# The 80-row tile of six projections computed in four column groups of TensorE

## The chip, the cores and the metric

One core of a Trainium2 chip runs the whole program in one launch. The metric is the device time of that launch in microseconds, the median of several runs. The core has five engines that run side by side and meet only at semaphores: TensorE (PE in the rows, PEld its weight loads), VectorE (DVE), ScalarE (ACT), GpSimd (POOL) and SyncE (SP, which here only starts DMA transfers). TensorE multiplies a stationary operand, up to 128 columns wide, with a moving one of up to 512 columns, and writes to PSUM, 128 partitions by 8 banks of 512 fp32; the stationary operand's columns become the output's partitions. VectorE and ScalarE take results from PSUM to SBUF.

## What is computed

The reference runs two layers of a streaming encoder over 592 tokens: 512 of a prompt, 64 of a sample and 16 meta tokens. Only the parts around the change are shown.

```python
def even_mixer(x, ...):                       # layer 0
    z = jnp.einsum('btd,de->bte', x, w_in)    # D_MODEL = 1024
    hq, hf, hi, hg, fq, fk, fv, ffg = jnp.split(z, [...], axis=-1)
    ...
    o_hg = rms_norm(o_hg, hg_norm_g).reshape(B, T, HG_VO) * jax.nn.sigmoid(hg)
    ...
    mixed = jnp.concatenate([o_hg, o_fox.reshape(B, T, FOX_W).astype(o_hg.dtype)], axis=-1)
    y = jnp.einsum('bte,ed->btd', mixed, w_out)
...
def trunk(...):
    for l in range(DEPTH):                    # DEPTH = 2
        ...                                   # y from even_mixer or odd_mixer (its w_out alike)
        x = layer_norm(ALPHA * x + y.astype(x.dtype), p['ln_mix_g'][l], p['ln_mix_b'][l])
        f = moe(x, ...)
        x = layer_norm(ALPHA * x + f, p['ln_ffn_g'][l], p['ln_ffn_b'][l])
```

Everything is fp32. Here `hi` (called v in the kernel), `hg` (g), `fk` and `fv` are 592 x 512 each with a contraction over 1024, and each of the two output projections (one a layer) is 592 x 1024 over 1024.

## The kernel before

**Tiles.** The 592 tokens are held feature-major in `xT` (128 partitions, 8 chunks of features, 592 tokens) and are cut into five token tiles, `TILES = [128, 128, 128, 128, 80]`. Tile 4, the 80 rows, holds the sample's 64 tokens and the 16 meta tokens.

**Token-major projections.** For v, g, fk and fv, `to_tokens` (L1067 to L1075) takes the tokens of a tile as the stationary operand and 512 columns of the weights as the moving one, and sums over 8 chunks: 8 matmuls to a tile, each of which is two records in the trace. The output projection of layer l, in `out_and_experts` (L1311), does the same for two halves of 512 columns into two banks (L1324); after tile i it transposes tile i - 1, which has been normalized by then (`normed_tile`).

**Order.** Each engine runs its own list as written. TensorE: the first forget projection, v tiles 0 to 4, the first q projection (L1084), g tiles 0 to 4; then 20 units of the recurrence with the other feature-major projections laid between them (L1190), before which it waits until g tiles 3 and 4 and v tile 4 are out of PSUM; then fk tiles, each followed by the transposes of the tile before (L1225); fv tiles; attention of layer 0, which waits for fv tile 4; the output projection; the router; 13 blocks of experts. Each block (`gate_up` L1420, `down` L1441) already multiplies in four column groups: four experts have 32 slots each, the stationary operand is 32 columns wide, and the output goes to partitions 32j to 32j + 31. Layer 1 has latent attention in between and then `out_and_experts(1)`.

**PSUM.** The eight banks are four pairs, and a ticket for each result says in which pair it lies. `claim` waits until the pair's last user has been read (`ps_free`), `filled` until TensorE is done (`pe_full`).

**Who empties PSUM.** ScalarE copies v (L1670), fk (L1665) and fv (L1720), and takes exp(-x) of g (L1678), one instruction for each tile. VectorE adds the residual to an output projection straight from PSUM, 1024 columns in one instruction (L2107, `stt` in `layer_norm_tile`), then takes the statistics and scales (L2110 to L2117); GpSimd computes the inverse root in between (L843, L844). SyncE starts the weight loads: the g weights when v tile 4 is done, experts 2 and 3 and part of 4 when tile 4 of the output projection is done.

## Time and profile before

| | us |
|---|---|
| median of 3 runs | 1290.17 |
| lowest and highest | 1289.34, 1294.49 |
| the profiled execution | 1288.5 |
| its span, first to last instruction | 1285.5 |
| TensorE busy (share of the span) | 1137.2 (88%) |
| VectorE | 568.5 (44%) |
| ScalarE | 263.5 (20%) |
| GpSimd | 221.2 (17%) |

The rows in the section after the next give times in microseconds from the span's start. A row of the timeline or of the chain stands for several instructions (x16: sixteen); its second number runs from the start of the first to the end of the last. The end of a matmul is modelled, and matmuls are pipelined: one of 512 columns is shown 0.59 us long while the next one starts after 0.43. In the shape 128*80 of a matmul the first number is the rows of the array that take part, the second the columns, that is the tokens.

### The profile page before, as it was taken

The page shows a single profiled execution, that of the slowest core. Times are in us where ns is not written, and L with a number is a line of the kernel's source. Part 1 is how long each engine was busy: PE and PEld are TensorE (multiplying, and loading weights), DVE is VectorE, ACT ScalarE, POOL GpSimd, SP SyncE. Part 2 cuts the span into 40 slices and gives each one's busy share as a digit, 9 for nine tenths or more (in the row PEclk, how much of TensorE's full clock was granted, in tenths as well). Part 3 has the DMA queues.
Part 4 walks back from the last instruction along what each step waited for, and adds up shares of the span by engine and source line. Part 5 has one row for each costly group of instructions (what it writes and reads, how often), then busy time and mean ns, then how long its engine had stood idle before and what let it go on. Part 6 is the DMA issues. An engine that isn't in the chain of part 4 may idle for free.

```text
span 1285.5 us, 16760 instructions
## 1 busy us (share of the span) xinstructions
PE 1137.2 (88%) x6333; PEld 611.3 (48%) x6333; DVE 568.5 (44%) x1254; ACT 263.5 (20%) x622; POOL 221.2 (17%) x382
## 2 busy tenths in 40 slices
PE   8999999999899939999839899999999975999965
PEld 4547777644654313333215446677574432333322
DVE  2079878610734435643365230450253344474226
ACT  1214334311420001111101312332331010111012
POOL 0106444421101211001062300000000210100114
PEclk9999999999999959999959999999999996999987
DMA  9103211261842277999582312000104246899935
GB/s 351 66 30 146 87 67 66 83 226 53 70 165 98 104 292 288 376 416 337 204 312 78 118 61 66 1 1 1 66 1 196 93 171 246 303 396 405 331 108 201
DMA packets 41821, 214.69 MB, mean 167 GB/s; under 512 B 4488, under 2 KB 6088, under 8 KB 32400
## 3 DMA queue, kind: packets, MB, share of 16 engines
q1 hardware_dynamic: 24288, 152.57, 30.4%
q0 software_dynamic: 17168, 60.27, 15.1%
q8 instruction: 51, 0.84, 0.3%
q10 hardware_dynamic: 288, 0.80, 0.2%
q14 instruction: 26, 0.21, 0.1%
HBM read 180.31 MB, written 33.29 MB: 166 GB/s over the span
## 4 chain that ended last, share of the span: by engine, by line
PE 79%; DVE 8%; issue 4%; DMA 4%; ACT 3%; POOL 1%; DVEq 0%; ACTq 0%; POOLq 0%; SPq 0%
PE pair L1420 12%; PE pair L1324 11%; PE pair L1073 11%; PE pair L1441 6%; PE pair L1084 5%; PE pair L1190 5%; PE pair L1256 5%; PE pair L1517 3%; PE pair L1293 3%; PE pair L1569 2%; DMA arena<-x_rows,ints 2%; PE pair L1406 2%; PE pair L1114 2%; PE pair L1549 2%; PE pair L1291 2%
## 5 line engine op out<-in xcount | busy, mean ns | idle before, releaser
L1073 PE MATMUL pair<-ring,xT 128*128 128x512 f32 (+1 forms) x320 | 138.8, 593 | 0.0
L1420 PE MATMUL pair<-ring,arena 128*32 128x512 f32 x608 | 130.2, 598 | 0.0
L1420 PE MATMUL pair<-arena 128*32 128x512 f32 x736 | 106.0, 631 | 8.1 <-issue 4.6
L1073 PEld LDWEIGHTS pair<-ring,xT 128*128 128x128 f32 (+1 forms) x320 | 57.7, 182 | 75.5 <-issue 75.1
L1190 PE MATMUL pair<-xT,ring 128*128 128x296 f32 x320 | 85.1, 421 | 6.1 <-ACT arena L1607 3.0
L843 POOL TENSOR_SCALAR small<-small 128x1 f32<-128x1 f32 (+3 forms) x45 | 17.2, 383 | 414.2 <-DVE small L2112 359.1
L865 POOL TENSOR_TENSOR arena<-arena 128x128 f32<-128x128 f32 x140 | 57.2, 443 | 155.4 <-PE pair L1116 86.6
L1256 PE MATMUL pair<-arena 128*128 128x264 f32 (+5 forms) x280 | 76.5, 402 | 2.6 <-issue 1.4
L2048 DVE TENSOR_REDUCE small<-pair 128x1 f32<-128x144 f32 (+4 forms) x40 | 22.4, 560 | 120.3 <-PE pair L1261 120.2
L1324 PE MATMUL pair<-ring,mixT 128*128 128x512 f32 (+1 forms) x160 | 72.1, 593 | 1.0 <-issue 1.0
L1190 PEld LDWEIGHTS pair<-xT,ring 128*128 128x128 f32 x320 | 60.4, 193 | 25.6 <-issue 9.2
L991 POOL DMA_INDIRECT arena<-x_rows,ints x26 | 26.4, 1014 | 268.6 <-PE pair L1406 164.6
L1324 PE MATMUL pair<-ring,xT 128*128 128x512 f32 (+1 forms) x160 | 71.9, 592 | 0.0
L2250 DVE COPY arena<-pair 128x256 f32<-128x256 f32 x26 | 11.0, 423 | 134.9 <-PE pair L1429 134.9
L1441 PE MATMUL pair<-ring,arena 128*32 128x512 f32 x304 | 65.3, 595 | 4.0 <-DVE arena L2250 4.0
L1420 PEld LDWEIGHTS pair<-arena 128*32 128x32 f32 x736 | 31.1, 116 | 68.6 <-issue 68.6
L1084 PE MATMUL pair<-arena,ring 128*128 128x296 f32 (+1 forms) x224 | 62.1, 438 | 0.0
L1420 PEld LDWEIGHTS pair<-ring,arena 128*32 128x32 f32 x608 | 34.0, 111 | 57.4 <-issue 57.4
L1517 PE MATMUL pair<-ring,xT 128*128 128x512 f32 (+3 forms) x160 | 59.2, 526 | 1.1 <-ACT xT L1598 1.1
L1420 PE MATMUL pair<-xT,arena 128*32 128x512 f32 x320 | 56.3, 592 | 0.0
L1598 ACT COPY xT<-pair 128x1024 f32<-128x1024 f32 (+1 forms) x15 | 14.2, 948 | 202.9 <-PE pair L1065 202.9
L2107 DVE SCALAR_TENSOR_TENSOR rb<-xr,pair 128x1024 f32<-128x1024 f32 (+1 forms) x10 | 12.2, 1221 | 95.8 <-PE pair L1324 95.8
(356 smaller groups left out, 1910.4 us busy)
## 6 DMA issues: line engine op xcount, KB each, us to landing
arena<-in_moe_w_gate_up SPq DMA_DIRECT2D x14, 2048.0 KB, 9.2
ring<-in_moe_w_gate_up SPq DMA_DIRECT2D x12, 2048.0 KB, 9.4
arena<-in_moe_w_down SPq DMA_DIRECT2D x14, 1024.0 KB, 9.6
y_rows<-arena SPq DMA_DIRECT2D x26, 512.0 KB, 8.5
ring<-in_moe_w_down SPq DMA_DIRECT2D x12, 1024.0 KB, 11.6
xT<-in_moe_w_gate_up SPq DMA_DIRECT2D x6, 2048.0 KB, 15.0
ring<-in_even_w_in SPq DMA_DIRECT2D x5, 2048.0 KB, 7.5
y_rows<-xr POOLq DMA_DIRECT2D x12, 512.0 KB, 8.6
```

Source lines behind the costliest of these rows:

```text
L865: last = pool.tensor_tensor(dst, both, mid, ALU.subtract)
L991: pool.indirect_dma_start(xg[:, e % 2, :], None, x_rows[2 * l], bass.IndirectOffsetOnAxis(ap=sloti[:, e:e + 1], axis=0)).then_inc(xg_in[e ...
L1073: last = pe.matmul(ps[0:P, 0:n], xT[:, k, 128 * i:128 * i + P], w[:, k, :], start=(k == 0), stop=(k == chunks - 1))
L1084: last = pe.matmul(ps[0:w.shape[2], 512 * s:512 * s + n], w[:, k, :], src[:, k, n * s:n * s + n], start=(k == 0), stop=(k == chunks - 1))
L1114: pe.matmul(ps[0:P, 128 * n:128 * n + P], gbuf[:, u % 2, n, 0:P], gbuf[:, u % 2, n, 0:P], start=True, stop=True)
L1190: last = pe.matmul(ps[0:w.shape[2], 512 * s:512 * s + n], w[:, k, :], xT[:, k, n * s:n * s + n], start=(k == 0), stop=(k == KD - 1))
L1256: last = pe.matmul(ps[0:P, lo:lo + cols], q_, k_, start=(c == 0), stop=(mask is None and c == len(lq) - 1))
L1293: last = pe.matmul(out, vb[j], pT[:, n % 2, 128 * j:128 * j + P], start=False, stop=(j == nb - 1))
L1324: last = pe.matmul(ps[0:P, 512 * half:512 * half + 512], mixed(k, i), w[:, k, :], start=(k == 0), stop=(k == KD - 1))
L1420: last = pe.matmul(bank[c, :], xgT[:, e % 2, k, c], expert_place(x)[0][:, k, :], start=(k == 0), stop=(k == KD - 1))
L1441: last = pe.matmul(psum[2][c:c + 32, 512 * half:512 * half + 512], hT[:, e % 2, 128 * k + c:128 * k + c + 32], expert_place(x)[1][:, k, 51 ...
L1517: last = pe.matmul(ps[0:P, lo:lo + n], xT[:, k, 128 * i:128 * i + P], w[:, k, :], start=(k == 0), stop=(k == KD - 1))
```

## The change

Tile 4 of the six projections v, g, fk, fv and the two output projections is multiplied in four column groups of 32. Its rows are cut into 0 to 31, 32 to 63 and 64 to 79 (`ROWS`). Groups 0 to 2 take one of these each and multiply it with the first three quarters of the weight's columns, 384 of 512. Group 3, whose output is on the partitions from 96 on, takes the last 128 columns for all three in turn; the result of row group r goes to columns 128r to 128r + 127 of the same bank (`moved`). For each chunk k the program issues one matmul for each of groups 0 to 2 and three for group 3, which counts through its own 24 pairs of row group and chunk. Other tiles stay as they are. The results are collected by four instructions where there was one: the 384 columns of all 80 rows, and three blocks of 128 columns from partition 96 on to the rows where they belong. For an output projection each of the four covers both halves.

```diff
+        ROWS = [(0, 32), (32, 64), (64, TILES[4])]
+
+        def moved(ps, r, lo=0, n=512):
+            a, b = ROWS[r]
+            return ps[96:96 + b - a, lo + n // 4 * r:lo + n // 4 * (r + 1)]
...
+            def last_tile(ps, w, tokens, lo=0):
+                K, n = w.shape[1], w.shape[2]
+                m = 3 * n // 4
+                for k in range(K):
+                    for a, b in ROWS:
+                        pe.matmul(ps[a:b, lo:lo + m], tokens(k)[:, a:b], w[:, k, 0:m],
+                                  start=(k == 0), stop=(k == K - 1))
+                    for t in range(3 * k, 3 * k + 3):
+                        r, c = divmod(t, K)
+                        a, b = ROWS[r]
+                        last = pe.matmul(moved(ps, r, lo, n), tokens(c)[:, a:b], w[:, c, m:n],
+                                         start=(c == 0), stop=(c == K - 1))
+                return last
...
+                if i == NT - 1:
+                    last_tile(ps, w, lambda k: xT[:, k, 128 * i:128 * i + P]).then_inc(pe_full.sem(key), 1)
+                    return
...
                     for half, w in ((0, w0), (1, w1)):
+                        if i == NT - 1:
+                            last = last_tile(ps, w, lambda k: mixed(k, i), 512 * half)
+                            continue
...
+            def token_rows(f, out, ps, i):
+                if i < NT - 1:
+                    return f(out, ps[0:128, 0:512])
+                f(out[:, 0:384], ps[0:TILES[i], 0:384])
+                for r, (a, b) in enumerate(ROWS):
+                    last = f(out[a:b, 384:512], moved(ps, r))
+                return last
...
-                copy(fks[0:P, i, :], filled(act, key)[0:P, 0:512]).then_inc(ps_free.sem(key), 1)
+                token_rows(copy, fks[0:P, i, :], filled(act, key), i).then_inc(ps_free.sem(key), 1)
...
-                stt(r, xr[0:P, b, :], ALPHA, filled(dve, key)[0:P, :], ALU.mult, ALU.add).then_inc(ps_free.sem(key), 1)
+                ps = filled(dve, key)
+                if i < NT - 1:
+                    added = stt(r, xr[0:P, b, :], ALPHA, ps[0:P, :], ALU.mult, ALU.add)
+                else:
+                    halves = lambda v: v.rearrange("p (h n) -> p h n", h=2)
+                    stt(halves(r)[:, :, 0:384], halves(xr[0:P, b, :])[:, :, 0:384], ALPHA,
+                        halves(ps[0:P, :])[:, :, 0:384], ALU.mult, ALU.add)
+                    for q, (lo, hi) in enumerate(ROWS):
+                        added = stt(halves(rb[lo:hi, b, :])[:, :, 384:512], halves(xr[lo:hi, b, :])[:, :, 384:512], ALPHA,
+                                    halves(ps[96:96 + hi - lo, :])[:, :, 128 * q:128 * q + 128], ALU.mult, ALU.add)
+                added.then_inc(ps_free.sem(key), 1)
```

The copies of v and fv and the exp of g go through `token_rows` as that of fk does. The places as they stand in the built programs follow; a shape is that of the output, and line numbers of the changed kernel are its own.

TensorE, tile 4 of v, between the other tiles of v (`ring` holds the weights, `xT` the tokens) and the q projection, before:

```order
L1095 MATMUL pair<-xT,mixT 128x296 x16
L1073 MATMUL pair<-ring,xT 128x512 x32
L1073 MATMUL pair<-ring,xT 80x512 x8
L1084 MATMUL pair<-xT,mixT 128x296 x16
L1073 MATMUL pair<-ring,xT 128x512 x32
```

The same place in the changed kernel, from chunk 5 on, where group 3 goes over to the 16 rows (in the five chunks ahead the rows of L1086 are one, `32x128 x3`):

```order
L1081 MATMUL pair<-ring,xT 32x384 x2
L1081 MATMUL pair<-ring,xT 16x384
L1086 MATMUL pair<-ring,xT 32x128
L1086 MATMUL pair<-ring,xT 16x128 x2
L1081 MATMUL pair<-ring,xT 32x384 x2
L1081 MATMUL pair<-ring,xT 16x384
L1086 MATMUL pair<-ring,xT 16x128 x3
L1081 MATMUL pair<-ring,xT 32x384 x2
L1081 MATMUL pair<-ring,xT 16x384
L1086 MATMUL pair<-ring,xT 16x128 x3
L1109 MATMUL pair<-xT,mixT 128x296 x16
```

The 8 matmuls of the tile have become 48, six to a chunk, at the same place in the list.

ScalarE, the exp of g tile 4 and what is behind it (L1636 is the exp of the recurrence's decays), before:

```order
L1636 ACTIVATE arena<-arena 128x896
L1678 ACTIVATE arena<-pair 128x512 x4
L1678 ACTIVATE arena<-pair 80x512
L1636 ACTIVATE arena<-arena 128x896 x2
L1645 COPY arena<-pair 80x128
```

And in the changed kernel:

```order
L1673 ACTIVATE arena<-arena 128x896
L1715 ACTIVATE arena<-pair 128x512 x4
L1715 ACTIVATE arena<-pair 80x384
L1715 ACTIVATE arena<-pair 32x128 x2
L1715 ACTIVATE arena<-pair 16x128
L1673 ACTIVATE arena<-arena 128x896 x2
```

Four instructions stand where one did, and the decays of the next unit are queued behind them.

VectorE, the residual sum and the statistics of tile 4 after an output projection, before:

```order
L2117 SCALAR_TENSOR_TENSOR rb<-rb,small,lng 128x1024
L2107 SCALAR_TENSOR_TENSOR rb<-xr,pair 80x1024
L2110 BN_STATS small<-rb 80x6
L2111 BN_STATS small<-rb 80x6
L2112 BN_AGGR small<-small 80x2
```

And in the changed kernel:

```order
L2165 SCALAR_TENSOR_TENSOR rb<-rb,small,lng 128x1024
L2150 SCALAR_TENSOR_TENSOR rb<-xr,pair 80x2x384
L2153 SCALAR_TENSOR_TENSOR rb<-xr,pair 32x2x128 x2
L2153 SCALAR_TENSOR_TENSOR rb<-xr,pair 16x2x128
L2158 BN_STATS small<-rb 80x6
```

The sum comes in four pieces, and the statistics wait for the last.

## Rows read from the trace of the kernel before

**Rows 1.** The page: busy time of TensorE; the chain that ended last, by engine

```profile
PE 1137.2 (88%) x6333; PEld 611.3 (48%) x6333; DVE 568.5 (44%) x1254; ACT 263.5 (20%) x622; POOL 221.2 (17%) x382
...
PE 79%; DVE 8%; issue 4%; DMA 4%; ACT 3%; POOL 1%; DVEq 0%; ACTq 0%; POOLq 0%; SPq 0%
```

**Rows 2.** The chain in order of time: start us, us, what

```profile
16.13 34.37 PE pair L1073 x80
...
276.06 6.88 PE pair L1073 x16
...
429.85 13.75 PE pair L1324 x32
443.72 1.23 DVE rb L2107
```

**Rows 3.** Timeline between two expert blocks: start us, us, engine, line, instructions

```profile
606.06 1.04 PE L1420 MATMUL pair<-ring,arena 128*32 128x512 f32 x8
...
607.03 0.44 PE L1429 MATMUL pair<-cst,arena 128*128 128x128 f32 x2
...
607.30 1.04 PE L1406 MATMUL pair<-cst,arena 128*128 128x128 f32 x8
...
608.27 0.63 PE L1441 MATMUL pair<-arena 128*32 128x512 f32 x3
...
608.29 0.62 PE L1441 MATMUL pair<-ring,arena 128*32 128x512 f32 x1
608.30 0.12 PEld L1441 LDWEIGHTS pair<-arena 128*32 128x32 f32 x3
...
608.73 0.60 PE L1441 MATMUL pair<-arena 128*32 128x512 f32 x3
```

**Rows 4.** Short passes: one group by shape, then timelines, L1167 in two windows

```profile
L1293 PE MATMUL pair<-arena 128*128 128x128 f32 x240 | 34.9, 275 | 0.8 <-issue 0.8
...
368.30 0.72 PE L1293 MATMUL pair<-arena 128*128 128x128 f32 x5
...
1054.75 0.28 PE L1167 MATMUL pair<-xT,vecs 128*32 128x80 f32 x4 [0.78 <-ACT xT L1598]
...
1054.75 0.48 PE L1167 MATMUL pair<-xT,vecs 128*32 128x80 f32 x16 [0.78 <-ACT xT L1598]
...
104.72 0.39 PE L1134 MATMUL pair<-arena 80*16 80x128 f32 x2
```

**Rows 5.** Reads of PSUM by ScalarE and VectorE: groups by shape, then timelines

```profile
L1747 ACT COPY arena<-pair 128x128 f32<-128x128 f32 x12 | 3.1, 256 | 0.5
...
282.96 0.58 ACT L1665 COPY arena<-pair 80x512 f32<-80x512 f32 x1 [6.23 <-PE pair L1073]
283.44 0.58 ACT L1715 COPY arena<-pair 128x512 f32<-128x512 f32 x1
...
746.64 0.42 DVE L2418 TENSOR_TENSOR arena<-pair,cst 128x256 f32<-128x256 f32 x1 [1.15 <-PE pair L1549]
746.99 0.41 DVE L2419 TENSOR_TENSOR arena<-pair,cst 128x256 f32<-128x256 f32 x1
```

**Rows 6.** Timeline of TensorE behind g tile 4 and fk tile 4

```profile
93.64 4.22 PE L1190 MATMUL pair<-xT,ring 128*128 128x296 f32 x16 [0.83 <-ACT arena L1678]
...
284.17 0.47 PE L1225 MATMUL pair<-cst,arena 80*128 80x80 f32 x4 [0.81 <-ACT arena L1715]
```

**Rows 7.** Timeline of TensorE: the transposes of tile 4 behind the output projection

```profile
449.76 0.77 PE L1065 MATMUL pair<-cst,rb 80*128 80x80 f32 x8 [0.51 <-DVE rb L2117]
```

**Rows 8.** The chain again: gate and up of the first expert block, and a later one

```profile
474.88 8.79 PE pair L1420 x64
...
600.23 6.87 PE pair L1420 x64
```

**Rows 9.** Windows: stretch; PE, PEld, DVE, ACT, POOL busy; PEclk, DMA, GB/s

```profile
474.90:478.30 3.40, 3.40 (x17) 0.91 (x21) 0.00 (x0) 0.00 (x0) 0.32 (x1) 0.50 0.46 154
...
600.30:606.90 6.60, 6.60 (x64) 1.82 (x56) 0.69 (x1) 0.58 (x1) 1.05 (x2) 1.00 0.97 318
```

More of the change, by code:

```diff
@@ L1669, in _ @@
                 P = TILES[i]
-                copy(hv[0:P, i, :], filled(act, ("v", i))[0:P, 0:512]).then_inc(ps_free.sem(("v", i)), 1)
+                token_rows(copy, hv[0:P, i, :], filled(act, ("v", i)), i).then_inc(ps_free.sem(("v", i)), 1)
                 if i == 1:
@@ L1677, in _ @@
                 P, key = TILES[i], ("g", i)
-                act.activation(hgate[0:P, i, :], filled(act, key)[0:P, 0:512], ACT.Exp, scale=-1.0).then_inc(ps_free.sem(key), 1)
+                token_rows(lambda out, ps: act.activation(out, ps, ACT.Exp, scale=-1.0), hgate[0:P, i, :],
+                           filled(act, key), i).then_inc(ps_free.sem(key), 1)
             for u in range(20):
@@ L1719, in _ @@
                     act.wait_ge(*vz_sb["fox"])
-                copy(fv[0:P, i, :], filled(act, key)[0:P, 0:512]).then_inc(ps_free.sem(key), 1)
+                token_rows(copy, fv[0:P, i, :], filled(act, key), i).then_inc(ps_free.sem(key), 1)
             def att_exp(n):
```

## The prediction

> **What bounds the kernel now.** I read the page first, for which engine the end of the run hangs on, then the chain of waits in order of time, for where the six projections lie in it, then the timeline around the expert blocks, because they are the only work before the change that multiplies in four column groups. TensorE is busy 88% of the span and 79% of the chain that ended last is its work [rows 1]. The chain runs through tile 4 of all six projections: v, g and fv each stand in it as one unbroken piece of 80 records, 34.4 us, fk as five of 16, and tile 4 of an output projection (both halves of the columns) ends a piece of 13.75 us that hands straight over to VectorE [rows 2]. With the halves that makes eight times 512 columns. So time taken from TensorE in tile 4 comes off the run, less what the engine that empties PSUM needs more.
>
> Each fp32 matmul is two records in the trace, which I call passes. The old tile 4 of one projection half is 8 chunks x 2 passes = 16 passes of 512 columns, and takes 6.88 us, 0.429 us a pass, with 80 of 128 columns of the array in use [rows 2]. A tile of 128 rows takes the same time, so the 48 idle columns are what the change goes for.
>
> **TensorE, one projection half.** After the change three groups of 32 columns (the last with 16 rows) hold the tile's rows and take 384 of the 512 weight columns, and the fourth group takes the other 128 for the three row groups in turn. Groups 0 to 2 have 16 passes of 384 columns: 0.429 x 384/512 = 0.322 us each, 5.15 us. Group 3 has 8 x 3 x 2 = 48 passes of 128 columns. The price of such a pass decides the case. Five passes of 128 columns in a row end 0.72 us after the first one starts, and one lasts 0.275, so they start 0.111 apart; eight transposes give (1.04 - 0.27)/7 = 0.110 [rows 3, 4]. Those are full-width passes. In column groups the nearest thing is the router's partial sums, four groups at once, 80 columns: 4 passes take 0.28 us and 16 take 0.48, so three further rounds cost 0.20, 0.067 each, which is 80/512 of 0.429 [rows 4]. So loading 32 new columns of weights does not show even in a pass shorter than ours. I take 0.109 (128/512 of 0.429 and 2 ns). Below it there is only the bare 0.107; above it stands the pair of 128-column passes with a 16-column load, the first after a wait, 0.39 - 0.27 = 0.12 apart [rows 4]. Group 3 is then the longest with 48 x 0.109 = 5.24 us, and one half costs 5.24 in place of 6.87.
>
> Entering and leaving column groups costs too. The last round of the gate and up weights starts at 606.49 (two rounds of 0.43 from 606.06), the next full-width pass would start at 606.92 and does so at 607.03; the last of the eight transposes starts at 608.07 and the next round of column groups at 608.27, not 608.18. That is 0.11 less the 0.02 by which the groups of a round lie apart, and 0.09: 0.09 each way [rows 3]. The Trainium skill (TensorEngine Tiling (Array Packing), Key Properties) says that a change of tiling mode drains the engine; the trace agrees.
>
> Do four groups of unlike length run side by side? In the built program the two passes of a matmul stand together, group after group. Yet at 608.27 the first passes of all four groups start within 0.02 us and the second ones follow 0.46 later [rows 3]: a group's second pass waits while later matmuls of other groups go ahead. The changed stream needs this to reach a few instructions further, since group 3 must start its second matmul while the second passes of the others still wait. If it reached no further than now, group 3 would fall behind once, by part of a chunk, and catch up in its own time: the wide groups leave it no gap.
>
> **The engines that empty PSUM.** For v, g, fk and fv ScalarE makes four instructions of one. 80x512 takes 0.58 and 128x128 takes 0.256, so 384 columns take 0.47, and the four take 0.47 + 3 x 0.256 = 1.24, or 1.24 - 3 x 0.10 = 0.94 if they overlap as the copies at 282.96 and 283.44 do, which lie 0.48 apart at 0.58 long [rows 5]. I take +0.36, at most +0.66. After v nothing waits for it: TensorE has q to do. After g TensorE waits 0.83 for this instruction now [rows 6], so all of it is on the path. After fk the next copy is behind it in ScalarE's queue, and TensorE waits for that copy, 0.81 [rows 6]: on the path. After fv the attention waits for it in the same way: on the path.
>
> For the output projections VectorE makes four of one. 80x1024 takes 1.22. 256 columns take 0.42, so a column costs (1.22 - 0.42)/768 = 1.04 ns, 768 columns 0.95, and the four 0.95 + 3 x 0.42 = 2.22. Instructions of 256 columns that read PSUM start 0.33 to 0.35 apart at 0.42 long [rows 5], so the four take some 1.94. I take +0.72, at most +1.0. It is on the path: VectorE starts at 443.72, when TensorE ends tile 4, and TensorE later waits 0.51 for the normalized tile [rows 2, 7]. That wait also says that TensorE's own work in between (tile 3's transposes and router sums) is 0.5 us short of binding; it moves forward by more than VectorE's, so it stays hidden.
>
> **The sum.** v: 6.87 - 5.24 - 0.19 = 1.44 saved. g: the way out of column groups falls into a wait, 6.87 - 5.24 - 0.09 - 0.36 = 1.18. fk: 1.44 - 0.36 = 1.08. fv as g, 1.18. Each output projection: 13.74 - 10.48 - 0.09 - 0.72 = 2.45, twice 4.90. Together 9.8 us. The profiled execution took 1288.5 us (span 1285.5), so it would be 1278.7; against the median of the runs, 1290.17, it is **1280.4 us**. The DMA loads behind tile 4 (the g weights behind v, experts 2 and 3 behind the output projection) are started by the tile's end and move with it, so I count nothing for them. The unknowns: ScalarE and VectorE up to 1.5 us more; a 0.001 us change of the narrow pass is 48 x 8 x 0.001 = 0.38 us, so 0.12 would give back 4.2. Then there is TensorE's clock. The granted clock is 0.50 (1.2 of 2.4 GHz) while the first expert block begins, straight behind the router's long waits, and 1.00 in a later one; that first block costs 8.79 us where a later one costs 6.87 [rows 8, 9]. It is the first of five such pieces in the chain. Work that arrives earlier may meet the return of the clock sooner or later than now; each can move by up to the 1.9 us that it costs, and I allow 3 us either way in total.
>
> **Rivals.** *The narrow passes are not free of their loads.* Nowhere in this kernel does one group load weights three times while the other three are in one pass. If in group 3 each load (0.11 [rows 3]) comes before its pass and not beside the one before, a pass costs 0.22, a half 48 x 0.22 = 10.5, and the run gets 8 x (10.5 - 5.24) = 42 us longer than my sum: about **1322 us**. It decides from 0.109 + 9.8/384 = 0.134 us a pass on: dearer than that, the change loses. Against it: at 608.30 the loads for the second passes start 0.03 after the first passes have [rows 3], and the 0.067 rounds. The Trainium skill (TensorE: Matmul & The Clock Gate, Part 3) states that a weight load overlaps a running matmul only where the row groups differ, and here they never do; by that rule this rival would be the forecast, and the load at 608.30 speaks against the rule.
>
> *Passes start strictly in the program's order.* Then a chunk is a wide pass, three times one more beside the next group's first, and six narrow ones behind: 3 x 0.322 + 5 x 0.109 = 1.51 us, a half 12.1, and 8 x (12.1 - 5.24) = 55 on top of my sum: about **1335 us**. By the same order the gate and up block would take 8 x 4 x 0.429 = 13.7 us, and it takes 6.87 [rows 8]. The Trainium skill (the same page and part) says that matmuls start and end in program order with no reordering; that rule gives this rival, and the 6.87 denies it.
>
> *Part of it comes off.* Narrow passes at 0.12 to 0.13, or a short stall at each chunk because group 3 runs ahead or behind, or the clock comes back later after a router: with a pass of 0.12 (4.2) and 1.4 from the clock on 1280.4 it is **1286 us**, within 0.5% of before.
>
> **How the numbers follow.** About 0.5% is what a measurement of this kernel can tell from no change; it is 6.45 us, the forecast is 9.8. The sum as made has 0.68, and 0.62 of it ends more than 0.5% faster, the rest is lost to the clock's share. Part of it comes off has 0.18. The serial loads have 0.10, strict order 0.04. So faster 0.62, same 0.24, slower 0.14. The range runs from 1280.4 less 5 (clock, and overlaps better than taken) to 1290, which takes in the third rival and a narrow pass of nearly 0.13; what is left out is mainly the two rivals beyond it.
>
> **What would show it.** The timeline of tile 4 of v: 96 records of TensorE in about 5.4 us, the narrow ones 0.109 apart, the wide ones 0.32; a gap at every eighth part would be the third rival, narrow ones 0.22 apart the first. In the chain of waits v's piece shortens from 34.37 to about 32.9 us and the piece of 13.75 to about 10.6. TensorE's wait before L1190 near 92 us grows from 0.83 to about 1.2, and VectorE needs about 1.9 us from the end of an output projection to the statistics. I am wrong if these hold and the total does not fall, which could only be later waits (for expert weights, or the clock) that grow by the same.

## The result and the profile after

The changed kernel takes **1280.19 us**, the kernel before, run on the same chips, 1292.44: a ratio of 0.9915 with an interval of 0.9892 to 0.9939, 11.0 us less (7.9 to 14.0). The forecast was 1280.4, which was 9.8 us less than the 1290.17 of the three runs of before known then; the range was 1275.5 to 1290. The profiled execution took 1280.19 as well, its span is 1277.3 (1285.5 before).

The page of the changed kernel, busy time and the chain by engine (before: [rows 1]):

```profile
PE 1125.8 (88%) x6973; PEld 632.0 (49%) x6973; DVE 570.7 (45%) x1260; ACT 266.7 (21%) x634; POOL 223.3 (17%) x382
...
PE 77%; DVE 9%; issue 5%; DMA 5%; ACT 3%; SPq 1%; POOL 0%; DVEq 0%; ACTq 0%; POOLq 0%
```

TensorE is busy 11.4 us less with 640 records more. The timeline of TensorE at the start and the end of tile 4 of v (start us, us, engine, line, instructions) shows that the four groups run side by side:

```profile
43.26 0.59 PE L1098 MATMUL pair<-ring,xT 128*128 128x512 f32 x1
43.78 0.52 PE L1081 MATMUL pair<-ring,xT 128*32 128x384 f32 x3
43.80 0.52 PE L1086 MATMUL pair<-ring,xT 128*32 128x128 f32 x3
44.13 0.49 PE L1081 MATMUL pair<-ring,xT 128*16 128x384 f32 x3
44.15 0.49 PE L1086 MATMUL pair<-ring,xT 128*32 128x128 f32 x3
...
48.74 0.49 PE L1086 MATMUL pair<-ring,xT 128*16 128x128 f32 x3
49.16 8.24 PE L1109 MATMUL pair<-xT,mixT 128*128 128x296 f32 x32
```

Rounds of wide passes start at 43.78, 44.13 and from there 0.322 apart; beside each stand three narrow ones of group 3. Three narrow passes last 0.49 from first start to last end and one lasts 0.27, so they start 0.11 apart. The tile takes 49.16 - 43.78 = 5.38 us, the way out of column groups in it; the old one took 6.87 [rows 2]. The way in is 43.78 - 43.26 - 0.43 = 0.09. All four token-major tiles that take part show 5.38, and the output projection 10.62 where it had 13.75 [rows 2] (from 426.74 to the transposes at 437.36, in the rows further down).

What ScalarE needs behind g, and TensorE's waits behind g, fk and fv, from the timeline of the changed kernel (the first two waits answer to [rows 6]):

```profile
90.92 1.34 ACT L1715 ACTIVATE arena<-pair 80x384 f32<-80x384 f32 x4 [4.78 <-PE pair L1086]
...
92.56 0.74 PE L1215 MATMUL pair<-xT,ring 128*128 128x296 f32 x2 [1.67 <-ACT arena L1715]
...
282.43 0.47 PE L1250 MATMUL pair<-cst,arena 80*128 80x80 f32 x4 [1.49 <-ACT arena L1753]
...
317.63 0.48 PE L1281 MATMUL pair<-arena 128*128 128x144 f32 x2 [1.85 <-ACT arena L1634]
```

The waits were 0.83, 0.81 and, behind fv, 1.14 (at 320.15 in the trace of the kernel before); they have grown by 0.84, 0.68 and 0.71, where the forecast put 0.36 on each.

The chain of waits has a piece that the kernel before doesn't have, the load of the g weights behind v (chain in order of time: start us, us, what; the tile of v stands between the first two rows):

```profile
16.11 27.73 PE pair L1098 x64
...
49.26 8.47 DMA ring<-in_even_w_in
57.77 27.73 PE pair L1098 x64
```

### The profile page after: what moved, and what is told of

Its sections match the earlier page's. It is cut to its first block, busy times and chain, and to the rows that moved or that the text cites. A ratio compares the mean times of both kernels' runs of the same rounds, so it can differ in the third digit from the quotient of the medians.

```text
span 1277.3 us, 18058 instructions
## 1 busy us (share of the span) xinstructions
PE 1125.8 (88%) x6973; PEld 632.0 (49%) x6973; DVE 570.7 (45%) x1260; ACT 266.7 (21%) x634; POOL 223.3 (17%) x382
## 4 chain that ended last, share of the span: by engine, by line
PE 77%; DVE 9%; issue 5%; DMA 5%; ACT 3%; SPq 1%; POOL 0%; DVEq 0%; ACTq 0%; POOLq 0%
PE pair L1448 12%; PE pair L1098 9%; PE pair L1352 9%; PE pair L1469 6%; PE pair L1215 5%; PE pair L1109 5%; PE pair L1281 5%; PE pair L1545 4%; PE pair L1318 3%; PE pair L1597 2%; PE pair L1086 2%; DMA arena<-x_rows,ints 2%; PE pair L1434 2%; PE pair L1139 2%; DMA ring<-in_even_w_in 2%
## 5 line engine op out<-in xcount | busy, mean ns | idle before, releaser
L1098 PE MATMUL pair<-ring,xT 128*128 128x512 f32 x256 | 111.3, 593 | 0.9 <-DMA ring<-in_even_w_in 0.9
L1098 PEld LDWEIGHTS pair<-ring,xT 128*128 128x128 f32 x256 | 48.1, 190 | 59.8 <-issue 57.9
L1215 PEld LDWEIGHTS pair<-xT,ring 128*128 128x128 f32 x320 | 60.4, 193 | 25.8 <-issue 9.4
L1352 PE MATMUL pair<-ring,mixT 128*128 128x512 f32 x128 | 57.7, 593 | 1.0 <-issue 1.0
L1352 PE MATMUL pair<-ring,xT 128*128 128x512 f32 x128 | 57.5, 592 | 0.0
L1109 PEld LDWEIGHTS pair<-arena,ring 128*128 128x128 f32 x224 | 42.4, 190 | 18.1 <-issue 6.7
```

Source lines behind the costliest of these rows:

```text
L1098: last = pe.matmul(ps[0:P, 0:n], xT[:, k, 128 * i:128 * i + P], w[:, k, :], start=(k == 0), stop=(k == chunks - 1))
L1109: last = pe.matmul(ps[0:w.shape[2], 512 * s:512 * s + n], w[:, k, :], src[:, k, n * s:n * s + n], start=(k == 0), stop=(k == chunks - 1))
L1215: last = pe.matmul(ps[0:w.shape[2], 512 * s:512 * s + n], w[:, k, :], xT[:, k, n * s:n * s + n], start=(k == 0), stop=(k == KD - 1))
L1352: last = pe.matmul(ps[0:P, 512 * half:512 * half + 512], mixed(k, i), w[:, k, :], start=(k == 0), stop=(k == KD - 1))
```

## The experiments

Where a median is given, it stands beside that of the kernel before in the same job, and the interval is of the ratio. Line numbers are each kernel's own.

**e1: the four input projections alone.** Tile 4 of the output projections is as before.

```diff
-                        if i == NT - 1:
-                            last = last_tile(ps, w, lambda k: mixed(k, i), 512 * half)
-                            continue
...
-                if i < NT - 1:
+                if True:
                     added = stt(r, xr[0:P, b, :], ALPHA, ps[0:P, :], ALU.mult, ALU.add)
```

> Only v, g, fk and fv have their tile 4 in column groups; the two output projections are as before. My theory (each tile gives back its own passes less its emptying, and nothing else): the profile of the changed kernel shows 1.4 us off at v, 0.7 at g, 0.65 at fk and 0.8 at fv, 3.5 in all, against 4.9 in my sum; the time should fall by 3 to 5 us. Rival (the gain is not in the tiles but in how later work meets TensorE's clock and the expert weights): the time falls by 8 us or more, or not at all, and not in step with the tiles.

Measured: 1288.52 against 1290.17, 0.9988 (0.9968 to 1.0007): 1.6 us less, 4.1 less to 0.9 more. The stages in the trace have their gain: tile 4 takes 5.38, and TensorE begins to transpose tile 3 of fk at 280.31 where it began at 282.76. So the question was whether something later takes the gain; e11 takes it up.

**e2: the output projections alone.**

```diff
-                if i == NT - 1:
-                    last_tile(ps, w, lambda k: xT[:, k, 128 * i:128 * i + P]).then_inc(pe_full.sem(key), 1)
-                    return
...
-                if i < NT - 1:
-                    return f(out, ps[0:128, 0:512])
+                if True:
+                    return f(out, ps[0:TILES[i], 0:512])
```

> Only the two output projections have their tile 4 in column groups. My theory: 2.1 us off each by the changed kernel's trace (2.45 in my sum), 4 to 5 us in all; with the run that has only v, g, fk and fv it adds up to the whole change. Rival (later waits give the gain): the two parts do not add up to the 11 us measured for the whole, or one of them has it all.

Measured: 1284.20 against 1290.17, 0.9937 (0.9914 to 0.9961): 8.1 us less (5.0 to 11.1; the medians lie 6.0 apart), where my sum had 4.9 for this part. It looks like more than I had counted, if only just outside the interval, and e12 and e13 ask why.

**e4: the narrow passes behind all wide ones.** How far ahead of waiting matmuls does a free group go?

```diff
                 for k in range(K):
                     for a, b in ROWS:
                         pe.matmul(ps[a:b, lo:lo + m], tokens(k)[:, a:b], w[:, k, 0:m],
                                   start=(k == 0), stop=(k == K - 1))
-                    for t in range(3 * k, 3 * k + 3):
-                        r, c = divmod(t, K)
...
+                for t in range(3 * K):
+                    r, c = divmod(t, K)
...
```

> The same 96 passes a tile half, but all wide ones of groups 0 to 2 are issued first and the 48 narrow ones of group 3 behind them. It tells how far TensorE looks past passes that wait. My theory (the reach is limited, some 10 to 20 passes): the narrow ones start only when the wide ones are nearly through, so a half takes 5.2 + 5.2 us less some 1 to 2 us of overlap at the end, 8.4 to 9.4 in place of 5.3, and the kernel is 25 to 33 us slower than the changed one, 14 to 22 slower than before. Rival 1 (the reach is far, each group has its own list): no difference from the changed kernel. Rival 2 (strict order between groups, which only looks concurrent where groups alternate): a half takes 10.4 and the kernel is 41 us slower than the changed one.

Measured: 1312.35 against 1290.17, 1.0163 (1.0127 to 1.0199). TensorE's timeline in tile 4 of v:

```profile
43.73 0.52 PE L1081 MATMUL pair<-ring,xT 128*32 128x384 f32 x3
...
47.30 0.81 PE L1081 MATMUL pair<-ring,xT 128*32 128x384 f32 x6
47.65 0.51 PE L1086 MATMUL pair<-ring,xT 128*32 128x128 f32 x3
...
53.00 0.52 PE L1109 MATMUL pair<-xT,mixT 128*128 128x296 f32 x1
```

Group 3 stands idle until 47.65. At 47.62 the thirteenth of the 16 rounds of wide passes has started, and within 0.03 us the first narrow pass starts. So three rounds, nine wide passes, were still waiting when a matmul behind them could go. Nine is not the whole rule, though. In the output projection of e4 the wide passes of the second half stand behind the 48 narrow ones of the first:

```profile
449.88 0.71 PE L1086 MATMUL pair<-ring,xT 128*16 128x128 f32 x5
450.32 0.52 PE L1081 MATMUL pair<-ring,mixT 128*32 128x384 f32 x3
450.42 0.49 PE L1086 MATMUL pair<-ring,xT 128*16 128x128 f32 x3
```

Here groups 0 to 2 stand idle until only three narrow passes wait, and in layer 1 it is the same (1059.40, three narrow ones from 1059.50 on). One reading fits both counts: a matmul can go when no group ahead of it has more than three passes waiting, three times three in tile 4 of v and once three here. The counts are measured, the reading per group is an inference from them. The tile of v takes 9.27 us, 3.89 more than in the changed kernel; over four tiles and two output projections (18.02 against 10.62) that is 30.4 us, and the medians of the two kernels lie 32.2 apart. A group does go ahead of others that wait, but only so far, and the close interleaving by chunk in the changed kernel is what the gain hangs on.

**e5: three groups, nothing moved.** Groups 0 to 2 take all 512 columns, the fourth stays empty.

```diff
                     for a, b in ROWS:
-                        pe.matmul(ps[a:b, lo:lo + m], tokens(k)[:, a:b], w[:, k, 0:m],
+                        last = pe.matmul(ps[a:b, lo:lo + n], tokens(k)[:, a:b], w[:, k, :],
                                   start=(k == 0), stop=(k == K - 1))
-                    for t in range(3 * k, 3 * k + 3):
...
```

> Three column groups with all 512 columns each and no fourth group: nothing is moved to partition 96, and PSUM is emptied by one instruction as before. It has the column groups' own cost and none of the gain. My theory (the gain is only that 384 columns take the place of 512): each tile costs 16 x 0.429 us and 0.09 us at each change of mode, so the kernel is 1 us slower than before at most, no difference that can be measured. Rival (column groups are faster in themselves, for instance by shorter weight loads): it keeps a good part of the 11 us.

Measured: 1292.64 against 1290.17, 1.0019 (0.9997 to 1.0041). Tile 4 of v runs from 43.86 to 50.85, 6.99 us:

```profile
43.34 0.59 PE L1093 MATMUL pair<-ring,xT 128*128 128x512 f32 x1
43.86 0.62 PE L1081 MATMUL pair<-ring,xT 128*32 128x512 f32 x3
...
50.85 0.52 PE L1104 MATMUL pair<-xT,mixT 128*128 128x296 f32 x1
```

The way in is again 43.86 - 43.34 - 0.43 = 0.09, and the way out 6.99 - 6.87 = 0.12. Six visits cost 1.3 us, so column groups by themselves give nothing; the gain is the 128 columns that go to the fourth.

**e6: passes of 64 columns in group 3.** 96 passes in place of 48, with the same columns in all.

```diff
-                    for t in range(3 * k, 3 * k + 3):
-                        r, c = divmod(t, K)
+                    for t in range(6 * k, 6 * k + 6):
+                        rq, c = divmod(t, K)
+                        r, q = divmod(rq, 2)
+                        c0, c1 = (n - m) // 2 * q, (n - m) // 2 * (q + 1)
```

> Group 3 does the same columns in 96 passes of 64 columns to a tile half in place of 48 of 128. It measures the floor under a narrow pass. My theory (weight loads hide beside the pass before, in a group of its own too): 0.054 to 0.058 us a pass, group 3 stays at 5.2 to 5.6 us a half and the time within 2 us of the changed kernel. Rival (a load of 32 columns, shown 0.11 us long, bounds a pass from somewhere between 64 and 128 columns on): up to 0.11 a pass, 10.5 us a half, and 40 us longer in all.

Measured in one run: 1280.71, beside a median of 1289.52 for the kernel before. TensorE's timeline:

```profile
43.97 0.49 PE L1081 MATMUL pair<-ring,xT 128*32 128x384 f32 x3
44.00 0.50 PE L1088 MATMUL pair<-ring,xT 128*32 128x64 f32 x6
```

One such pass lasts 0.22, so six in 0.50 start 0.056 apart: 64/512 of 0.429 is 0.054, and 2 ns. The whole tile takes 5.50 in place of 5.38, 0.0025 us for each pass more. A weight load that is twice as frequent does not show, so the rival of serial loads is out, with a factor of two to spare.

**e8: finer pieces on ScalarE and VectorE.** The forecast let each piece begin before the one ahead was done. The trace of the changed kernel denied it, so here the 384 columns are copied in three pieces, each moved block in two, and VectorE's 768 columns in two.

```diff
-                f(out[:, 0:384], ps[0:TILES[i], 0:384])
+                for q in range(3):
+                    f(out[:, 128 * q:128 * q + 128], ps[0:TILES[i], 128 * q:128 * q + 128])
                 for r, (a, b) in enumerate(ROWS):
-                    last = f(out[a:b, 384:512], moved(ps, r))
+                    for c in (0, 64):
+                        last = f(out[a:b, 384 + c:448 + c], moved(ps, r)[:, c:c + 64])
...
+                    for o in (0, 512):
+                        stt(r[:, o:o + 384], xr[0:P, b, o:o + 384], ALPHA, ps[0:P, o:o + 384], ALU.mult, ALU.add)
```

> Pieces cut finer, with the same data: ScalarE takes the 384 columns as three of 128, and each moved block as two of 64; VectorE takes the 384 columns of the two halves as two instructions. It asks why the pieces did not overlap as I took them to (0.27 apart at 0.26 long on ScalarE, 0.96 at 0.95 on VectorE), while the rope products of another stage start 0.34 apart at 0.42 long. Guess 1 (a change of the first partition between source and destination, 96 to 0, stops the overlap): the three of 128 columns that stay on their partitions start about 0.16 apart, the moved ones do not overlap. Guess 2 (a change of the partitions from one instruction to the next stops it): the second of two moved ones with the same partitions starts early, the others do not. Guess 3 (fewer than 128 partitions stop it): none overlaps.

Measured in one run: 1277.69, beside 1289.52. First ScalarE behind v, then VectorE behind the output projection, from the timeline of e8:

```profile
49.26 0.59 ACT L1633 COPY arena<-pair 80x128 f32<-80x128 f32 x3 [4.79 <-PE pair L1086]
49.86 0.32 ACT L1636 COPY arena<-pair 32x64 f32<-32x64 f32 x2
...
50.19 0.32 ACT L1636 COPY arena<-pair 32x64 f32<-32x64 f32 x2
...
438.65 1.02 DVE L2153 SCALAR_TENSOR_TENSOR rb<-xr,pair 80x384 f32<-80x384 f32 x2 [5.13 <-PE pair L1086]
439.68 1.29 DVE L2155 SCALAR_TENSOR_TENSOR rb<-xr,pair 32x256 f32<-32x256 f32 x3
```

Three copies of 0.264 that write the same 80 partitions take 0.59: they start 0.16 apart. Two of 0.20 to the same 32 rows take 0.32: 0.11 apart. But the next pair, which reads the same PSUM partitions and writes other rows, starts at 50.19, when the one ahead is over (49.86 + 0.32 = 50.18). VectorE is alike: two sums of 0.547 over the same rows take 1.02, 0.47 apart; three of 0.42 to three different row ranges take 1.29, 0.43 apart. So the pieces that keep their first partitions overlap, and those that change one do not. The step from the wide copies to the first block changes only the first partition that is read (0 to 96; both write from row 0), the step from block to block on ScalarE only the one that is written, and either is enough. The length of the range does not decide it: the copies at 282.96 and 283.44 write 80 and 128 rows, both from 0, and overlap [rows 5]. The moved blocks always change one. The Trainium skill (VectorE: DVE Perf Modes, The DRAIN you can't avoid) says that an operation of VectorE does not start until the one ahead has emptied the pipe, but that one which is not held starts earlier. By the section that it points to, Two Vector instructions with no wait between them, an operation is held when an input or its output starts in another group of 32 partitions than in the instruction ahead. VectorE's starts agree with that: 0.47 apart at 0.55 long within the same groups, 0.43 apart at 0.42 long across them.

**e7: half of the residual sum early.** VectorE sums the first 512 columns while TensorE multiplies the second, which go to the other bank.

```diff
+                            if half == 0:
+                                last.then_inc(wo_half.sem, 1)
...
+                    dve.wait_ge(*wo_half[l])
+                    for h in range(2):
+                        if h == 1:
+                            filled(dve, key)
+                        o = 512 * h
+                        stt(r[:, o:o + 384], xr[0:P, b, o:o + 384], ALPHA, ps[0:P, o:o + 384], ALU.mult, ALU.add)
+                        for q, (lo, hi) in enumerate(ROWS):
+                            added = stt(rb[lo:hi, b, o + 384:o + 512], xr[lo:hi, b, o + 384:o + 512], ALPHA,
+                                        ps[96:96 + hi - lo, o + 128 * q:o + 128 * q + 128], ALU.mult, ALU.add)
```

> VectorE sums the first half (512 columns) of an output projection's tile 4 while TensorE multiplies the second, with a signal of its own: eight pieces in place of four, four of them behind the end. My theory (the pieces lie on the path): behind TensorE's end remain 0.55 + 3 x 0.29 = 1.4 us in place of 2.25, so the router begins 0.85 us earlier in each layer and the time falls by some 1.7 us, seen in the trace and hardly in the medians. Rival (TensorE's transposes and router sums of the other tiles are as late): nothing changes at the transposes of tile 4, whose wait for VectorE goes below 0.6 us.

Measured: 1278.15 against 1289.52, 0.9920 (0.9896 to 0.9944). VectorE is done 1.49 us behind TensorE's tile in place of 2.29, and the wait for tile 4's transposes is back to 0.52 [rows 7]; the total is the changed kernel's within the interval. So 0.8 us less on VectorE, twice, bought nothing that shows in four runs.

**e9: the moved blocks early too.** e7, and for v, g, fk and fv the first two row blocks of group 3 go to the second bank of the pair. ScalarE takes them when two thirds of the tile are done.

```diff
+        def placed(ps, r):
+            a, b = ROWS[r]
+            o = 512 + 128 * r if r < 2 else 0
+            return ps[96:96 + b - a, o:o + 128]
...
+                        if done and t == 2 * K - 1:
+                            last.then_inc(done, 1)
...
+                act.wait_ge(*early[key[0]])
+                for r, (a, b) in enumerate(ROWS):
+                    if r == 2:
+                        filled(act, key)
+                    last = f(out[a:b, 384:512], placed(ps, r))
+                return f(out[:, 0:384], ps[0:TILES[i], 0:384])
```

> Group 3 finishes its first two row blocks after two thirds of the tile. Here they are written to the second bank of the pair and their copies (v, fk, fv) and exp (g) run while TensorE is on the third; for an output projection VectorE sums the first half while TensorE multiplies the second. Left on the path behind a tile: for ScalarE one block and the 384 columns, two instructions whose partitions differ, so without overlap 0.26 + 0.48 = 0.74 us in place of 1.29; for VectorE 0.55 + 3 x 0.30 = 1.49 in place of 2.29. Theory (these engines' time behind a tile is on the path, as the four waits show): g, fk and fv 0.55 each and two output projections 0.8 each, 3.2 us less than the changed kernel, about 1277 where that has 1280. TensorE's tile stays at 5.38 us. Rival (it is off the path or the early reads disturb TensorE's passes): the same time as the changed kernel or more, and a half of a tile longer than 5.38.

Measured: 1277.08 against 1289.19, 0.9900 (0.9881 to 0.9918). In its timeline behind g ScalarE has two instructions left and TensorE waits 1.01 where the changed kernel waits 1.67:

```profile
90.71 0.77 ACT L1728 ACTIVATE arena<-pair 16x128 f32<-16x128 f32 x2 [0.78 <-PE pair L1092]
...
91.68 0.49 PE L1223 MATMUL pair<-xT,ring 128*128 128x296 f32 x1 [1.01 <-ACT arena L1728]
```

TensorE's tiles stay at 5.38, so the early reads cost it nothing. The 0.66 (behind fv 0.60, 1.52 against 2.12 from the last start) are there in the trace; their sum of under 2 us does not show in the total.

**e10: the changed kernel again**, as it is, in the same job.

> The changed kernel as it is, beside e9 and e11, since a few microseconds are to be told apart. Both theories: 0.9915 of the kernel before, within its interval of 0.9892 to 0.9939.

Measured: 1277.52 against 1289.19, 0.9902 (0.9882 to 0.9921). e9 is 0.4 us below it. The means lie 0.3 apart, and by the scatter of their 5 and 6 runs I estimate some 2.4 us of doubt either way: the expected 3.2 are not there, but the up to 2 us of the three ScalarE waits could be, unseen.

**e11: the kernel of e1 again.**

> The kernel of e1 once more: v, g, fk and fv in four groups, the output projections as before. It came out only 1.6 us faster, where the stages sum to some 4. Theory (the stages keep their gain, and the rest was TensorE's clock, whose mean was 0.950 in e1's runs against 0.953 of the kernel before): runs of equal mean clock are 4 to 5 us apart, and the median is 2 to 5 us below that of before, 0.996 to 0.998. Rival (a later wait takes the gain of the inputs): again 1.6 us or less, at an equal clock too.

Measured: 1284.70 against 1289.19, 0.9967 (0.9956 to 0.9979), 4.3 us less (2.7 to 5.7). A straight line through each kernel's runs (span over mean granted clock) puts e11 at a clock of 0.950 4.0 us and e1 4.9 us below the kernel before of the same job; against one line through the kernel before of all jobs it is 5.5 and 3.4. The inputs keep their gain. That e1 showed only 1.6 goes with a lower mean clock in its runs, 0.950 against 0.953; why its runs had it is not shown.

**e12 and e13: VectorE longer.** The first statistics of tile 4 are computed four times more in the changed kernel, once more in the kernel before; nothing else changes.

```diff
                 st = lst[0:P, b, :]
+                if i == NT - 1:
+                    for _ in range(4):
+                        chain(dve.bn_stats(st[:, 0:6], src[:, 0:512]))
```

> The changed kernel, with VectorE's first statistics of tile 4 computed four more times behind each output projection, some 0.7 us each, 2.9 us more on VectorE; the result is the same. Theory (cover that ends): TensorE goes on from the end of tile 4 to the first rows of the experts in 28.65 us in the kernel before and in 28.65 and 28.29 in the changed one, whose VectorE is 1.0 longer there, because the rows are gathered behind 9.4 MB of weights that start when tile 4 ends and last 24 us. In the changed kernel the weights end just as the gather is issued (462.1 and 463.1 us), so the cover is used up: the stretch grows by 2.4 to 2.9, to 30.7 to 31.5, in both layers. Rival 1 (VectorE is covered further): it stays under 29.1. Rival 2 (VectorE is on the path, as the prediction had it): it grows by the full 2.9.

> The kernel before, with the first statistics of tile 4 computed once more behind each output projection, some 0.7 us more on VectorE; the result is the same. Theory (the weights that start with the end of tile 4 cover it): from the end of tile 4 to the first rows of the experts TensorE takes the 28.65 us of the kernel before (28.1 to 29.1 in all kernels so far). Rival (VectorE is on the path, as the prediction had it): 29.35 in layer 0 and 29.3 in layer 1.

Measured: e12 1283.67 against 1287.24, 0.9955 (0.9936 to 0.9974); e13 1291.86, 1.0021 (1.0003 to 1.0040). What they were made for is the stretch from the end of tile 4 to the first rows of the experts. Timelines of TensorE and GpSimd there: the kernel before, the changed kernel, e12.

```profile
443.42 1.04 PE L1065 MATMUL pair<-cst,rb 128*128 128x128 f32 x8
...
468.23 0.97 POOL L991 DMA_INDIRECT arena<-x_rows,ints  x1 [0.68 <-DVE ints L2223]
...
472.07 0.45 PE L1406 MATMUL pair<-cst,arena 128*128 128x128 f32 x1 [4.71 <-DMA arena<-x_rows,ints]
```

```profile
426.74 0.52 PE L1081 MATMUL pair<-ring,mixT 128*32 128x384 f32 x3
...
437.36 1.09 PE L1072 MATMUL pair<-cst,rb 128*128 128x128 f32 x8
437.57 0.95 DVE L2150 SCALAR_TENSOR_TENSOR rb<-xr,pair 80x768 f32<-80x768 f32 x1 [5.13 <-PE pair L1086]
438.53 1.29 DVE L2153 SCALAR_TENSOR_TENSOR rb<-xr,pair 32x256 f32<-32x256 f32 x3
...
444.66 0.77 PE L1072 MATMUL pair<-cst,rb 80*128 80x80 f32 x8 [1.42 <-DVE rb L2165]
...
463.12 0.97 POOL L998 DMA_INDIRECT arena<-x_rows,ints  x1 [0.69 <-DVE ints L2271]
...
466.00 0.45 PE L1434 MATMUL pair<-cst,arena 128*128 128x128 f32 x1 [3.76 <-DMA arena<-x_rows,ints]
```

```profile
438.90 1.09 PE L1072 MATMUL pair<-cst,rb 128*128 128x128 f32 x8
...
468.12 0.97 POOL L998 DMA_INDIRECT arena<-x_rows,ints  x1 [0.69 <-DVE ints L2274]
...
471.10 0.45 PE L1434 MATMUL pair<-cst,arena 128*128 128x128 f32 x1 [3.85 <-DMA arena<-x_rows,ints]
```

From these and their like, in us from the start of tile 3's transposes, layer 0 and layer 1 (the second gather is that of the rows of the first experts):

| kernel | tile 4's transposes | second gather issued | TensorE has the rows |
|---|---|---|---|
| before | 6.34, 6.34 | 24.81, 24.53 | 28.65, 28.56 |
| e13 | 7.07, 7.07 | 25.42, 25.54 | 28.86, 28.36 |
| changed | 7.31, 7.31 | 25.76, 25.78 | 28.65, 28.57 |
| changed again, e10 | 7.31, 7.31 | 25.49, 25.83 | 28.29, 28.64 |
| e9 | 6.41, 6.40 | 24.89, 24.74 | 28.46, 28.34 |
| e2 | 7.31, 7.31 | 26.34, 26.09 | 29.06, 28.90 |
| e12 | 10.22, 10.21 | 29.22, 29.22 | 32.20, 31.85 |

With the gather issued anywhere from 24.5 to 25.8 the rows are there at 28.3 to 28.9 (28.1 to 29.2 with e6 and e7); from 26 on they come later with it, 2.6 to 3.0 us behind. Windows of the same stretch (stretch; PE, PEld, DVE, ACT, POOL busy; PEclk, DMA share, GB/s), of the kernel before, the changed one and e12, show what holds the early ones up:

```profile
443.40:468.00 24.60, 7.56 (x94) 4.86 (x92) 17.14 (x59) 2.78 (x5) 3.48 (x4) 0.66 0.96 395
468.00:472.00 4.00, 0.00 (x0) 0.00 (x0) 0.00 (x0) 0.00 (x0) 0.97 (x1) 0.50 0.77 247
```

```profile
437.40:462.00 24.60, 7.30 (x90) 4.71 (x90) 17.74 (x59) 2.79 (x5) 3.05 (x4) 0.68 0.96 396
```

```profile
464.00:466.00 2.00, 0.27 (x5) 0.22 (x5) 1.48 (x7) 0.00 (x0) 0.00 (x0) 0.50 0.00 0
466.00:471.00 5.00, 0.57 (x10) 0.43 (x10) 1.39 (x6) 0.00 (x0) 2.19 (x2) 0.50 0.48 128
```

For 24.6 us from the end of tile 4 the DMA engines are 96% busy at 395 GB/s with the experts' weights, which SyncE starts at that end. The first gather, 1.9 us ahead of the second, is issued while they run. In e12 the DMA share is 0.00 from 464 to 466: the weights are through, nothing covers VectorE any more, and its 2.9 us come out as 3.3 to 3.6. (The half that is over 2.9 arises ahead of the gather's issue, 29.22 against 25.76; I haven't traced it.) The theory expected up to 31.5 and got 31.85 and 32.20, but rival 1, under 29.1, is out. Rival 2, the full 2.9, can't be told from the theory by e12; what speaks against it is e13 and the row of the changed kernel, where VectorE is longer and the stretch is not. The total agrees with the two stretches: e12 is 5.8 us below the kernel before where the changed kernel is 11.0 and 12.6 below, and the stretches have grown by 6.8 together. In e13 the stretch is 28.86 and 28.36, on the mean 28.61 as before. Its total is nevertheless 2.7 us higher, and the interval just excludes no change; in its profiled execution the excess over the kernel before arises in the attention ahead of the edit (56.2 us from its first matmul to the output projection, against 51.9), where the granted clock was 0.72 from 350 to 360 us. That is one execution, so where the 2.7 of the medians come from stays open.

## Why the prediction was right, and where its steps were not

**TensorE: right to a few hundredths.** Narrow passes 0.109 apart, a half 5.38 where the sum had 5.24 + 0.09, the way in 0.09, the way out 0.12. The tile of v saves 1.40 (6.87 - 5.38 - 0.09), forecast 1.44. Both strong rivals are dead: loads hide even under passes of 64 columns (e6), and the groups run at unlike paces. "If it reached no further than now, group 3 would fall behind once": e4 measured the reach, nine passes of three groups or three of one. The Trainium skill (TensorE: Matmul & The Clock Gate, Part 3) has no reordering of matmuls at all. That holds in part: with the narrow passes 48 passes behind, most of the tile went in program order, and 30 us were lost.

**ScalarE: the term was mis-sized.** "1.24 - 3 x 0.10 = 0.94 if they overlap as the copies at 282.96 and 283.44 do": those two keep their first partitions, read and written; each of the three blocks here changes one, and e8 shows that then nothing overlaps. Copies take 1.29 in place of 0.58, +0.71 where I took +0.36, and said at most +0.66. g is worth 0.66 (forecast 1.18), fk 0.65 (1.08), fv 0.78 (1.18), all three from the start of tile 4 to the end of the wait above: 1.3 us less than forecast.

**VectorE: the size was off, and the place.** Four pieces take 2.26, +1.02 (2.26 against 1.24) where I took +0.72 and at most +1.0, for the same reason. But "it is on the path" was wrong: I followed VectorE to the transposes of tile 4, whose wait did grow from 0.51 [rows 7] to 1.42, and did not go on to the gather 18 us later, which stands behind the weights. The stretch is 28.65 before and 28.65 after. So an output projection is worth what TensorE saves, 13.73 - 10.62 - 0.09 = 3.02, and not 2.45. e7 and e9, which take VectorE's time back, have the rows at 28.1 to 28.5, hardly sooner; e12 shows that the cover ends where the changed kernel now stands.

**The loads: half right.** That the weights behind tile 4 "are started by the tile's end and move with it" is what makes the output projections worth more. Behind v I counted nothing for the g weights, whose load had ended 0.6 us before TensorE needed them. In the profile after it took 8.5 us from issue to landing where it had 7.2, and TensorE waited 0.38 for it; with the switch to g it takes 0.75 of the gain. Over the fourteen profiles the landing takes 7.1 to 7.6 in five (the kernel before, e2, e5, e6, e13) and 8.4 to 8.9 in nine (the changed kernel, e1, e4, e7 to e12), with the same 2 MB. What sets the nine apart is a packet on another queue, which the profile calls instruction, by its name the program's own code. The changed kernel from 54.0 to 54.4 us:

```profile
q8 instruction: 1, 0.02, 15.2%
```

In all nine this packet falls into the load (between 54.0 and 55.5 us, in e4 between 58.4 and 58.8, as its load is 4 us later). In the kernel before, e2, e5 and e13 there is none during the load, and in e6 it comes ahead of it, between 48.4 and 48.8. The DMA engines from 48.5 to 59.5 us in 40 slices, the changed kernel and e6:

```profile
GB/s 0 0 0 0 0 0 715 60 179 0 357 536 298 477 417 477 357 357 536 357 477 417 477 357 477 238 0 60 0 60 0 0 0 0 0 0 0 0 0 0
```

```profile
GB/s 60 0 0 0 0 0 715 238 0 60 238 655 179 715 119 715 179 596 357 357 536 357 596 238 655 119 0 0 0 0 0 0 0 0 0 0 0 0 0 0
```

In both the bulk of the load is through at 55.6, but in the changed kernel single packets still move until 56.7, 1.1 us later, and the landing is 1.2 us later. From the first pass of q to the first of g TensorE takes 7.97 us in the kernel before, 8.61 in the changed kernel and 8.08 in e6. So the new instructions most likely cost most of the 0.75 us by where their code is fetched. No run moved that packet and nothing else, so the cause is argued and not shown.

**The sum.** By stages: 1.40 + 0.66 + 0.65 + 0.78 + 2 x 3.02 - 0.75 = 8.8 us; forecast 9.8, measured 11.0 (7.9 to 14.0) and, in e10, 12.6 (10.2 to 15.2). Two errors of 1.3 and 1.1 us, one on each side, made the forecast look better than its steps, and that 1280.19 lies only 0.2 from it is luck. The two profiled executions are 8.2 us of span apart, which the stages account for; the last two to four us of the medians lie in no stage that the change touches. Profiles of one and the same stage scatter by that much: over these kernels the attention of layer 0 takes 51.2 to 56.2 us up to the output projection, and the expert blocks between the second and the eleventh transposes of a layer 108.9 to 113.6, with the clock's returns in them. I allowed 3 us for that, and can't say more.

## What to carry to other kernels

A tile that fills 5/8 of the array's columns can be cut into column groups and its idle group fed with a share of the others' moving columns, if the matmuls of all groups are issued interleaved, so that no group ever has more than some three passes waiting ahead of another group's next one. Price the collecting instructions at their full length when the first partition that they read or write is another than in the one ahead. And when an engine's time grows, follow it to the next thing that a DMA delivers: it may already wait there for a transfer that started with the event you moved forward.

## What was not expected of the hardware

- A group's matmul starts ahead of nine waiting passes of three other groups, and no further (first narrow pass 0.03 us after the last of the first 39 of 48 wide ones), but ahead of only three waiting passes of one other group (450.32 us in e4).
- In a column group a pass of 64 columns costs 0.056 us and one of 128 0.109, with new weights for every one: 2 ns over columns times 0.84 ns (e6).
- ScalarE starts a copy of 128 columns 0.16 after one like it to the same partitions, at 0.26 long; one that reads or writes from another first partition starts only at its end (e8). VectorE: 0.47 at 0.55, against 0.43 at 0.42.
- ScalarE and VectorE read one bank of a pair while TensorE writes the other, and its passes stay 0.109 and 0.322 apart (tile times of 5.38 and 10.62 in e9 and e7).
- A 2 MB load landed after 7.1 to 7.6 us without a packet of the instruction queue inside it (five profiles) and after 8.4 to 8.9 us with one (nine profiles).
